# Two of five token tiles of the expert input finished by ScalarE and GpSimd during the routing instead of by VectorE behind it

## The reference

```python
h = modulate(rms_norm(xp, norm2_g[l]), sh2, sc2)     # h * (1 + scale) + shift
xp = xp + g2[:, None, :] * moe(h, w_router, router_bias, w_e_gate[l], w_e_up[l], w_e_down[l])

def moe(h, ...):
    scores = sigmoid(t @ w_router)                   # 16 experts in 4 groups
    # best group of 4, then the top 2 experts inside it; weights normalised
    gate, up = t @ w_gate[e], t @ w_up[e]            # 1024 -> 256 for each expert
    return sum_e (silu(gate) * up * combine) @ w_down[e]
```

## Time and profile before

| | us |
|---|---|
| median of the three runs shown | 1919.79 (1919.49 to 1919.86) |
| profiled execution, device time | 1922.21 |
| profiled execution, span of the trace | 1920.1 |
| PE busy | 1724.7 (90%) |
| DVE busy | 956.3 (50%) |
| ACT busy | 720.2 (38%) |
| POOL busy | 501.9 (26%) |
| PE's share of the chain of waits that ended last | 34% of the span |

### The profile page before, as it was taken

One profiled execution on the slowest core, in us unless ns is written; L12 is line 12 of the kernel. 1 busy time (PEld: TensorE's weight loads), 2 busy tenths in 40 slices (PEclk: granted clock), 3 DMA queues, 4 the chain that ended last, 5 costly groups with the idle time before them and its releaser, 6 DMA issues. The chain is left out here.

```text
span 1920.1 us, 34707 instructions
## 1 busy us (share of the span) xinstructions
PE 1724.7 (90%) x13363; PEld 1353.8 (71%) x13363; DVE 956.3 (50%) x1849; ACT 720.2 (38%) x1394; POOL 501.9 (26%) x268
## 2 busy tenths in 40 slices
PE   6999999989999996988679999888899999787993
PEld 4899966679999974322278998567899998622232
DVE  4275477785667434111283753766756662601114
ACT  4453365553343431111254434655534342211113
POOL 1303510055546402000111133300654562200004
PEclk8999999999999997999889999999999999889996
DMA  7512277834342417997442221000323231779855
GB/s 278 196 45 67 89 255 247 272 119 132 134 153 66 166 72 311 359 337 283 140 169 103 67 67 37 1 1 6 105 67 99 67 132 68 297 297 401 297 176 197
DMA packets 170647, 305.95 MB, mean 159 GB/s; under 512 B 12530, under 2 KB 123250, under 8 KB 169716
## 3 DMA queue, kind: packets, MB, share of 16 engines
q1 hardware_dynamic: 146352, 227.07, 34.2%
q10 hardware_dynamic: 18372, 55.69, 8.0%
q0 software_dynamic: 5760, 20.97, 2.9%
HBM read 517.87 MB, written 41.68 MB: 291 GB/s over the span
## 5 line engine op out<-in xcount | busy, mean ns | idle before, releaser
L2462 PE MATMUL psum<-xw,h_T 128*32 128x512 f32 x1792 | 208.1, 609 | 26.8 <-DMA xw<-w_expert 24.6
L182 PE MATMUL psum<-whi,h_hi 128*128 128x256 f32 x720 | 210.2, 292 | 0.5 <-ACT v_tok L1012 0.5
L818 POOL TENSOR_TENSOR wlo<-raw,whi 128x2048 fp32r<-128x2048 f32 x25 | 115.3, 4612 | 361.3 <-ACT whi L898 361.3
L182 PE MATMUL psum<-whi,h_lo 128*128 128x256 f32 x720 | 203.6, 283 | 0.0
L182 PE MATMUL psum<-wlo,h_hi 128*128 128x256 f32 x720 | 203.6, 283 | 0.0
L2462 PEld LDWEIGHTS psum<-xw,h_T 128*32 128x32 f32 x1792 | 54.3, 112 | 159.9 <-issue 115.5
L978 ACT ACTIVATE prob<-psum,small_stats 128x640 f32<-128x640 f32 (+1 forms) x160 | 112.0, 705 | 135.4 <-DVE small_stats L1381 135.2
L1381 DVE TENSOR_REDUCE small_stats<-psum 128x1 f32<-128x640 f32 (+1 forms) x160 | 107.2, 711 | 98.1 <-PE psum L1685 73.6
L2359 DVE TENSOR_TENSOR gated_x<-psum,sig_x 128x256 f32<-128x256 f32 x28 | 11.9, 424 | 271.1 <-ACT sig_x L2073 271.1
L182 PEld LDWEIGHTS psum<-whi,h_hi 128*128 128x128 f32 x720 | 137.6, 191 | 3.0 <-issue 1.7
L182 PEld LDWEIGHTS psum<-wlo,h_hi 128*128 128x128 f32 x720 | 138.0, 192 | 0.0
(11 more groups left out here) (375 smaller groups left out, 4111.9 us busy)
## 6 DMA issues: line engine op xcount, KB each, us to landing
xw<-w_expert SPq DMA_DIRECT2D x376, 512.0 KB
xw<-w_expert ACTq DMA_DIRECT2D x296, 512.0 KB
raw<-w_in SPq DMA_DIRECT2D x46, 1024.0 KB, 5.4
wm_rest<-w_mod SPq DMA_DIRECT2D x40, 1024.0 KB, 5.3
y_rows<-y_sel SPq DMA_DIRECT2D x100, 128.0 KB, 6.5
h_sel<-h_rows ACTq DMA_DIRECT2D x22, 512.0 KB, 7.4
wm<-w_mod SPq DMA_DIRECT2D x4, 2048.0 KB, 16.8
raw<-w_out SPq DMA_DIRECT2D x8, 1024.0 KB, 5.0
```

The source lines that it names most:

```text
L182: mm = pe.matmul(dst, st, mv[q], start=start and n == 0, stop=stop and n == 2)
L818: pool.tensor_tensor(wlo[i % 2][:, :, :], raw[i % 2][:, :, :], whi[i % 2][:, :, :].bitcast(F32), ALU.subtract).then_inc(w_lo, 1)
L2462: mm = pe.matmul(psum[list_rows(q), i % 2, :], hT[i % 2][:, kc, q, :], xw[q][c][:, k * 512:(k + 1) * 512], start=(kc == 0), stop=(kc == KD ...
```

## The change

`POOL_ROWS = 2` is new. Tiles 0 and 1 of `h_tok` are no longer finished by VectorE. ScalarE, behind its eighth copy, multiplies each of the two by `rs2` in place; GpSimd, ahead of its wait for the routing, adds `shift_row` to each in place, and it is GpSimd that increments `k_d` for them. VectorE finishes tiles 2, 3 and 4 as before, and waits for both of GpSimd's additions ahead of tile 2. Everything else is unchanged.

```diff
+POOL_ROWS = 2
                 def _(pool):
+                    for t in range(POOL_ROWS):
+                        pool.wait_ge(k_a, KD + t + 1)
+                        pool.tensor_tensor(h_tok[:, t, :], h_tok[:, t, :], shift_row[:, int(t > 0), :], ALU.add).then_inc(k_d, 1)
                     pool.wait_ge(r_st, ROW_STEPS)
                     if first:
                         pool.wait_ge(s_rows0, 16 * 5)
...
                     for f in range(1, KD):
                         keep_turned(act, f)
+                    act.wait_ge(k_a, KD)
+                    for t in range(POOL_ROWS):
+                        act.activation(h_tok[:, t, :], h_tok[:, t, :], ACT.Copy, scale=rs2[:, t:t + 1]).then_inc(k_a, 1)
                     keep_h(0)
...
                     dve.wait_ge(k_a, KD)
-                    finish_rows(0)
...
                     for t in range(TT):
                         dve.tensor_tensor(pick[:, t, :]...).then_inc(k_pk, 1)
-                        if t + 1 < TT:
+                        if t == POOL_ROWS - 1:
+                            dve.wait_ge(k_d, POOL_ROWS)
+                        if POOL_ROWS <= t + 1 < TT:
                             finish_rows(t + 1)
```

## The result

| | us |
|---|---|
| before, median of 10 runs | 1919.63 (1916.35 to 1923.66) |
| changed, median of 10 runs | 1924.38 (1919.28 to 1926.80) |
| ratio, 95% interval | 1.0021 (1.0012 to 1.0031) |
| profiled execution of the changed kernel, device time | 1925.05 |
| its span | 1923.3 |

The change costs 0.21% by the ratio, some 4.0 us (the medians are 4.8 us apart); 3.5 us were forecast. The two profiled executions differ by 3.2 us in their spans.

The account below looks back on a forecast made before the run. All bytes in the DMA queue, weights first and the scatter behind, were taken to set the landing. 4.4 us for the late scatter less 0.9 us of pulls gave +3.5 us, 1923.3 us from 1919.8; range 1920.4 to 1926.2 us.

Parts of the forecast that it names:

- ScalarE's part costs nothing: ScalarE's two scalings, 1.15 us each, lie in its wait for keep_h(0) and cost nothing on that engine.
- GpSimd's additions stop the routing: GpSimd's SBUF-reading additions block VectorE's two-input routing steps; the last routing step ends 4.2 and 4.4 us later.
- Rival 2: Small routing steps slip past GpSimd and the DMA queue hides the scatter's shift: 0 us, 1919.8 us; chance 0.12.
- rival 3: No standstill, and the first scatter's earlier start is felt: −0.6 us, 1919.2 us; chance 0.02.
- The first scatter 2.9 and 3.1 us later: First scatter of each layer issued at 734.1 and 1667.85, 2.9 and 3.1 us later than before.
- the 0.85 us kept behind the last routing step: Gap from the last routing step to the first scatter, kept at 0.85 us from the old 0.89 and 0.78.
- the 0.7 us in each layer for the pace of the first two: Second scatter issued 1.99 us behind the first, a transfer takes 1.26 us: without weights 0.7 us lost per layer.
- The DMA queue hides a part and the engines stand empty for the rest: Weights ahead of the scatter hide part of its delay; engines then empty 0.6 to 1.2 and 1.8 to 2.35 us.
- The slow stretch of before's second layer, −0.6 us: From 1671 to 1675 engines moved 289 GB/s instead of 416, costing 1.2 us; it might vanish, half counted.
- The clock's −0.3 us: TensorE's shorter pause before the second tile might keep its clock up, gaining up to about 1 us; 0.3 counted.
- Rival 4: Scatter packets follow the issue at once, engines never run empty: +0.5 to +1.4 us, about 1921.0 us; chance 0.06.
- Rival 1: GpSimd's pace of issue sets the landing, so nothing of the late starts is hidden: +6.0, 1925.8 us; chance 0.12.

Follow-up runs that it names:

- e1: The changed kernel with the two additions made by VectorE instead of GpSimd, ScalarE still scaling; 1915.14 us against 1915.2 us before, ratio 0.9992.
- e2: The kernel before plus two unused GpSimd additions over 128x1024 that read SBUF, where the change has its additions; ratio 1.0024.
- e3: The kernel before plus four unused GpSimd memsets over 128x1024, which only write, where the change has its additions; ratio 0.9984.
- e6: The changed kernel with the last four first_down weight transfers moved behind the loads of the second and third list tile; ratio 0.9975 against before.
- e4: The changed kernel with one tile instead of two (POOL_ROWS = 1); ratio 0.9990 against the kernel before.
- e9: The kernel before with two GpSimd memsets between finish_rows(0) and the first scatter, so only the scatter starts later; ratio 1.0017.
- e10: The changed kernel timed again, nothing else altered; 1919.05 us, ratio 1.0009 against the kernel before.
- e7: The kernel before with finish_rows(0) put on VectorE ahead of the last ten routing steps instead of behind them; ratio 0.9983.

## Why the prediction was right

*ScalarE's part costs nothing.* Right: 2.19 us for two, 1.1 each against 1.15 forecast, and e1 has the time of before.

*GpSimd's additions stop the routing.* Right in place and in kind, a little less in size: 2.32 us each, two long steps in each layer, the last routing step 3.93 us late against e1 (23.41 and 19.48) where 4.2 and 4.4 were forecast. This was the step on which the forecast turned. Rival 2 (no standstill) and rival 3 fall with it, and e2 and e3 show the cause.

*The first scatter 2.9 and 3.1 us later.* Too much: 2.04 us (23.71 against 21.67) in the first layer, 2.1 against e1 in the second. The term that was mis-sized is the 0.85 us kept behind the last routing step. It belonged to `finish_rows(0)` and went with it; 0.30 us is left. Also the first issue became 0.6 us shorter, so that the tenth is only 1.5 us later (36.43 and 34.89), and the 0.7 us in each layer for the pace of the first two did not arise.

*The DMA queue hides a part and the engines stand empty for the rest.* Half right. The backlog hides, and more than forecast: no empty time arose (0.6 to 1.2 and 1.8 to 2.35 us were forecast). The start is earlier than assumed and the lead shorter, 2.1 us instead of 2.3 to 2.85, and 1.7 us with free engines (e6); in the window of the earlier trace rows itself the first packets come 1.7 us behind the issue at 1880.17, where the prediction had counted from the full flow. The 1 us to the first byte that the Trainium skill gives in "DMA: Bandwidth & Descriptors", section "Specifications", is shorter than the traces show, 1.7 to 2.3 us from the start of the issue to the first packets (e6 and e2).

*The slow stretch of before's second layer, −0.6 us.* Wrong in sign. I took it for something that might vanish, and it appeared in both layers. It goes with a late first scatter, 1.1 to 1.3 us in each layer. Up to it the changed kernel's transfers keep pace with e1's, so by this count it is what the change mainly pays with; no run removed it alone.

*The clock's −0.3 us.* It did not come, and its size had no row behind it. TensorE's wait for the second tile got shorter, and the granted clock fell in it all the same. Before, then the changed kernel with its clock (the number ahead of the last two), then e1, where the tile begins without a wait:

```profile
756.58 1.97 PE L2450 MATMUL psum<-ident,h_sel 128*128 128x128 f32 x8 [5.88 <-DMA h_sel<-h_rows]
...
756.73 1.97 PE L2458 MATMUL psum<-ident,h_sel 128*128 128x128 f32 x8 [3.58 <-DMA h_sel<-h_rows]
...
756.00:757.00 1.00, 0.27 (x2) 0.28 (x3) 0.00 (x0) 0.00 (x0) 0.00 (x0) 0.50 1.02 414
...
758.53 1.09 PE L2460 MATMUL psum<-ident,h_sel 128*128 128x128 f32 x8
```

From its first transposition to that of the third tile the second takes 16.56 and 17.31 us before (first and second layer), 17.85 and 17.28 us in the changed kernel, and 14.01 us in both layers of e1, where the clock is at 1.00 throughout. So behind a pause with the clock down the tile takes 2.5 to 3.8 us more, as much as the whole change, where the prediction had put the clock at up to about 1 us; how much of it is the clock alone no run separates. In e1 the pause lies ahead of `gate_up(0)` instead: ScalarE copies the first tile only 4.0 us behind the end of the product (at 747.75), and `gate_up(0)` runs at the lower clock while the second tile is still on its way. This is so in both layers of e1 to e4 and in neither of before, the changed kernel, e9 and e10, and no run shows why. Whole layers can therefore not be compared between these profiles, only the marks up to the landing and the ratios.

The sum: against the eight layers without the slow stretch (43.15 to 43.63, mean 43.4) the landing of the changed kernel is 0.6 and 0.7 us later in the first layer and 1.9 and 1.8 in the second, in its two profiles. That is 2.5 us for both layers, where 4.4 were forecast ahead of the pulls and 3.5 behind them; the timings say +4.0 and +1.7 us. Rival 4 (short lead, +0.5 to +1.4) had it right that the engines don't run empty, though the lead is not short, and lacks the slow stretch. Rival 1, +6.0, is not met in the time: of the 1.5 us of delay in the tenth issue 0.6 us come through in the first layer. In the second the landing is later by more than that delay. The forecast of +3.5 us has the standstill right, and the rest of its nearness is luck: the delay of the scatter and the empty time are too large, and the slow stretch is missing.

What stays open: why the landing moves more in the second layer than in the first at the same start of the scatter, although the transfers run on by much the same (from 42 to 43 us behind the constants 274 and 303 GB/s in the changed kernel, 45 and 49 in e1); what makes the packets slow in the stretch; and why e3 comes out slightly faster than before (0.9984), though it does nothing that could save time and its second layer has both the late product and the slow stretch. With that, 0.16% in a single ratio is not evidence here, and e7's 0.9983 and e4's 0.9990 are not claimed as gains. The same caution holds for e9's 1.0017, and for the change itself it leaves a cost of 0.1 to 0.2% that two timings and e2 point to.

## What to carry to other kernels

Before moving work to an engine that seems idle, look at what its neighbours do in those microseconds: a GpSimd addition that reads SBUF cost the chain of small two-operand VectorE steps beside it up to its whole length each time the two met, and a chain that something waits for is the worst place for it. Ask what the later stage waits for last: here it waits for bytes, so to start earlier brought nothing in the landing until the weights that nobody needed yet were moved behind the scatter. That move was worth about 6.5 us (ratio 0.9966); with the earlier start the ratios are 0.9961 and 0.9949, which the noise does not tell from it. And read a stretch of DMA by GB/s as well as by busy share.

## What the runs showed of the hardware that was not expected

- A DMA engine can count as busy and move little: for 4 to 5 us 301 and 311 GB/s instead of 417, with 0.49 us for a 4 KB packet of the weights in the first microsecond, against 0.15 us in e1.
- The first indirect DMA starts 0.30 us behind a small VectorE step that it waits for, and 0.78 to 0.89 us behind one over 128x1024; its issue takes 0.99 to 1.15 us in the first case and 1.63 to 1.76 us in the second, and 1.64 and 1.51 us in e9, where a memset is ahead of it. With free engines the first packets follow the end of the issue by 0.6 us (e2, e6).
- Memsets on GpSimd over 128x1024, 1.0 us each, leave VectorE's small two-operand steps alone (one step with a single input took 0.81 us at most), where additions of 1.9 to 2.3 us stop them for up to their whole length.
- A pause of TensorE ahead of the second tile cost more than the pause itself: the tile took 16.6 to 17.9 us with the granted clock down at 0.50, against 14.0 us in e1, where it stayed at 1.00.
